# Weighing a pair of items together in split precision, in a neighbourhood attention on one core

## The chip, the core and the metric

The kernel runs on one core of a Trainium2 chip. TensorE (PE) multiplies matrices from the on-chip memory SBUF into the accumulators PSUM (eight banks of 128 x 512 float32). VectorE (DVE), ScalarE (ACT) and GpSimd (POOL) compute on both or on SBUF; SyncE (SP) issues the DMAs. Each engine takes its own instructions strictly in order and waits for others on semaphores. The metric is the device time of one execution in microseconds; the median over runs is reported.

## The reference

One layer of a hybrid encoder, applied with shared weights to a prompt of 512 tokens and a sample of 1024 tokens, width 1024, all float32. The part that matters here is group B, a two-dimensional neighbourhood attention with 8 heads of 64 on a grid of 64 columns:

```python
def _neighbourhood_attention(q, k, v, rpb):
    ...
    r_start = jnp.clip(r_idx - kh // 2, 0, rows - kh)
    ...
    def row_fn(args):
        r, r0, q_row = args
        k_strip = lax.dynamic_slice_in_dim(kg, r0, kh, axis=1)
        v_strip = lax.dynamic_slice_in_dim(vg, r0, kh, axis=1)
        ...
        sc = jnp.einsum('bqhd,bikhd->bhqik', q_row, k_strip,
                        preferred_element_type=jnp.float32) * scale + bias[None]
        sc = jnp.where(col_ok[None, None, :, None, :], sc, -jnp.inf)
        p = jax.nn.softmax(sc.reshape(b, h, GRID_W, kh * GRID_W), axis=-1)
        ...
        return jnp.einsum('bhqik,bikhd->bqhd', p, v_strip)
```

Group A is a plain attention of 8 query heads over 2 key heads. Input projection, output projection, a gated MLP with a short convolution, an embedding gate and norms surround the two.

## The kernel before

The kernel runs in five stages; the attention is the second (`s2_*`), one function for each engine. Activations lie transposed, features on partitions. Between the stages all engines meet (`end_stage`). Matrix products outside group B's weighing are made from numbers in the type float32r, split into a rounded part and the remainder (names that end in H and L, `three_pass`).

The attention goes over 8 pairs of heads, four of group A (p = 0 to 3) and four of group B (p = 4 to 7). A pair is 24 items: two heads (`s`), each with three blocks (`g`: the prompt's 512 queries, the two halves of the sample's 1024), each of four items of 128 queries (`item`). An item of group B is two grid rows of 64 queries. The keys of the two rows overlap: `window` gives 512 keys where both rows have the same first key row ("edge", four blocks of 128), otherwise 576 ("mid", four blocks of 128 and one of 64). The three blocks of a head have 4 edge items; 2 edge and 2 mid; 2 mid and 2 edge.

`every_pair` calls `step` for m = 0 to 23 on each engine, so the order on each engine is fixed. In step m of group B:

- PE: `scores` of item m + 2 (L944, L945), `turn` of item m (L955: transposes of the probabilities into PSUM banks 4 and 5, after the exponential of m and once both banks are free), and in even steps `weigh_step` for items m - 2 and m - 1 (L979), from step 2 on; `norm_row` (L963) when m % 4 == 3. In steps 6 and 23 `values` (L929) turns the values of a head through the same two banks.
- ACT: `turned` copies bank 0 to PF (L1052), then `exps` of item m + 2 (L1042), and a `square` at steps 3, 19 and 23.
- DVE: `row_max` of item m + 2 (L1145: adds the bias table and finds the maximum), `turned_low` copies bank 1 to PF (L1154). If m % 4 == 1 it first reads out the finished output block, `out` (L1173 a copy of the accumulators to H, L1175 a multiplication by the inverse row sums), and takes `turned_low` ahead of `row_max`. Steps 3 to 5 and 18 to 20 also build bias tables (L1114, L1118, L1119).

Group A has the same steps, with both parts of the number: ACT copies both banks rounded to PTH (L1054), DVE then subtracts that from the bank and writes the remainder to PTL (L1158), and only that frees the bank (`t_hi`, `t_free`). Its `weigh` (L985) multiplies 128 x 128 values (64 columns rounded part, 64 remainder) with 256 columns of probabilities, two items at once, with PTH and with PTL. The output then comes in two halves of the partitions, so `out_copy` (ACT, L1061) takes one half out of PSUM and DVE adds the other (L1178) before it multiplies (L1182). In group B the values are float32 and 64 columns wide, the probabilities float32 and each item is weighed by itself in 128 columns; such a product is recorded twice in the trace.

## Time and profile before

| | |
|---|---|
| median of 3 runs | 2393.69 us (2391.83 to 2396.62) |
| profiled execution | 2396.31 us, its span 2394.2 us |
| mean granted TensorE clock | 0.975 |
| PE busy | 94% of the span |
| DVE, ACT, POOL busy | 68%, 34%, 12% |
| attention of group A, 372 to 672 us | PE busy 252.8 us of 300 |
| attention of group B, 672 to 905 us | PE busy 229.2 us of 233 |

The span runs from the first to the last instruction of the profiled execution; its time is a little more. Busy times are of one engine; matmuls overlap in a pipeline, so a busy PE need not be at its peak. The granted clock is the share of TensorE's full clock.

### The profile page before, as it was taken

The numbers are of one execution on the slowest core, as the hardware profiler recorded it, in microseconds if no ns is written. First come the engines' busy times: TensorE is split into PE (matmuls) and PEld (weight loads), VectorE is DVE, ScalarE is ACT, GpSimd is POOL, SyncE is SP. The second block draws the span as 40 slices with busy tenths as digits, with TensorE's granted clock in tenths as the row PEclk, the third lists the DMA queues.
The fourth block names the chain that finished last, engine by engine and source line by source line (L and its number), as shares of the span: only waits on it lengthen the run. The fifth ranks groups of instructions, "written<-read, shape, count | busy, mean of one in ns | idle before, by whom it ended". The sixth has DMA issues, their size and how long they took to land.

```text
span 2394.2 us, 30366 instructions
## 1 busy us (share of the span) xinstructions
PE 2247.9 (94%) x11036; PEld 1842.2 (77%) x11036; DVE 1621.3 (68%) x2130; ACT 802.1 (34%) x1281; POOL 297.7 (12%) x184
## 2 busy tenths in 40 slices
PE   6999998888899998998999999999999999987996
PEld 4777876777777787777888888888888888876884
DVE  7677427777766664774777776777777776775545
ACT  5222107666755553132121221122211222134223
POOL 6101010000000000540000000000000000014100
PEclk9999999999999998998999999999999999997997
DMA  5223445101045523010110000000000100010102
GB/s 164 101 83 115 152 143 121 27 13 26 15 89 108 108 54 123 35 36 18 36 35 26 35 35 26 35 35 26 35 35 26 35 35 26 35 53 18 44 27 105
DMA packets 51020, 137.47 MB, mean 57 GB/s; under 512 B 20240, under 2 KB 20752, under 8 KB 50960
## 3 DMA queue, kind: packets, MB, share of 16 engines
q1 hardware_dynamic: 50096, 135.55, 18.7%
q10 hardware_dynamic: 864, 1.13, 0.1%
q8 instruction: 37, 0.61, 0.1%
q14 instruction: 23, 0.19, 0.0%
HBM read 105.99 MB, written 30.67 MB: 57 GB/s over the span
## 4 chain that ended last, share of the span: by engine, by line
PE 68%; issue 23%; DVE 4%; POOL 2%; ACT 1%; DMA 1%; SPq 0%; POOLq 0%; ACTq 0%; DVEq 0%
PE ps L297 22%; PE ps L298 22%; PE ps L299 22%; POOL acc_a L915 1%; DVE WL L293 1%; POOL acc_b L915 1%; DVE NL L629 1%; PE ps L485 1%; PE ps L480 1%; DVE NL L1733 1%; DMA raw<-in_w 0%; DVE NL L1414 0%; DVE H L1905 0%; DMA ident<-in_ident 0%; PE ps L1244 0%
## 5 line engine op out<-in xcount | busy, mean ns | idle before, releaser
L297 PE MATMUL ps<-NH,WH 128*128 128x512 f32 x1896 | 756.8, 399 | 44.3 <-DVE WL L293 30.8
L298 PE MATMUL ps<-NL,WH 128*128 128x512 f32 x1896 | 743.5, 392 | 0.0
L299 PE MATMUL ps<-NH,WL 128*128 128x512 f32 x1896 | 742.8, 392 | 0.0
L297 PEld LDWEIGHTS ps<-NH,WH 128*128 128x128 f32 x1896 | 359.6, 190 | 129.4 <-issue 36.2
L298 PEld LDWEIGHTS ps<-NL,WH 128*128 128x128 f32 x1896 | 359.5, 190 | 79.9 <-issue 6.0
L299 PEld LDWEIGHTS ps<-NH,WL 128*128 128x128 f32 x1896 | 359.1, 189 | 76.0
L1665 DVE TENSOR_TENSOR H<-H,ps 128x512 f32<-128x512 f32 x480 | 305.4, 682 | 106.6 <-PE ps L299 106.6
L274 POOL TENSOR_TENSOR raw<-raw,gains 128x1024 f32<-128x1024 f32 x78 | 156.3, 2009 | 1378.7 <-DMA raw<-in_w 1368.2
L289 ACT ACTIVATE WH<-raw 128x1024 fp32r<-128x1024 f32 x104 | 109.9, 1057 | 574.9 <-PE ps L299 548.8
L955 PE MATMUL ps<-ident,PR 128*128 128x128 f32 (+1 forms) x1056 | 164.5, 285 | 49.8 <-DVE PTL L1158 45.0
L297 PE MATMUL ps<-MH,WH 128*128 128x512 f32 x504 | 197.9, 393 | 4.7 <-DVE H L1740 4.5
L299 PE MATMUL ps<-MH,WL 128*128 128x512 f32 x504 | 197.1, 391 | 0.0
L955 PEld LDWEIGHTS ps<-ident,PR 128*128 128x128 f32 (+1 forms) x1056 | 120.2, 141 | 99.8 <-DVE PTL L1158 54.8
L298 PE MATMUL ps<-ML,WH 128*128 128x512 f32 x504 | 196.9, 391 | 0.0
L293 DVE TENSOR_TENSOR WL<-raw,WH 128x1024 fp32r<-128x1024 f32 x104 | 133.8, 1287 | 52.4 <-ACT WH L289 52.4
L1647 DVE SCALAR_TENSOR_TENSOR ca<-u,convw,ca 128x511 f32<-128x511 f32 x88 | 113.1, 1343 | 43.3 <-ACT ca L1573 43.3
L1647 DVE SCALAR_TENSOR_TENSOR cg<-u,convw,cg 128x511 f32<-128x511 f32 x84 | 107.0, 1332 | 43.6 <-ACT cg L1573 43.6
L1137 DVE TENSOR_REDUCE nmax<-ps 128x1 f32<-128x1024 f32 (+1 forms) x96 | 99.2, 1033 | 41.6 <-PE ps L945 36.5
L297 PEld LDWEIGHTS ps<-MH,WH 128*128 128x128 f32 x504 | 94.9, 188 | 28.6 <-DVE H L1740 9.3
L1054 ACT ACTIVATE PTH<-ps 128x512 fp32r<-128x512 f32 (+1 forms) x192 | 94.1, 525 | 51.1 <-PE ps L955 50.0
L299 PEld LDWEIGHTS ps<-MH,WL 128*128 128x128 f32 x504 | 95.0, 189 | 19.8
L298 PEld LDWEIGHTS ps<-ML,WH 128*128 128x128 f32 x504 | 95.1, 189 | 19.3
(166 smaller groups left out, 2814.9 us busy)
## 6 DMA issues: line engine op xcount, KB each, us to landing
raw<-in_w SPq DMA_DIRECT2D x102, 512.0 KB, 3.2
xst<-in_xT SPq DMA_DIRECT2D x24, 256.0 KB, 4.3
H<-in_xT SPq DMA_DIRECT2D x8, 768.0 KB, 10.4
out_yT<-H SPq DMA_DIRECT2D x24, 256.0 KB, 2.1
qkh<-oqh SPq DMA_DIRECT2D x5, 768.0 KB, 3.3
qkl<-oql SPq DMA_DIRECT2D x5, 768.0 KB, 4.9
qkh<-obh SPq DMA_DIRECT2D x5, 768.0 KB, 3.5
qkl<-obl SPq DMA_DIRECT2D x5, 768.0 KB, 6.0
```

Of the source, the lines that this page charges most:

```text
L274: nc.gpsimd.tensor_tensor(v, v, g, ALU.mult).then_inc(w_sc, 1)
L289: nc.scalar.activation(WH[:, slot, :], raw[:, slot, :], ACT.Copy).then_inc(w_hi, 1)
L293: nc.vector.tensor_tensor(WL[:, slot, :], raw[:, slot, :], WH[:, slot, :].bitcast(F32), ALU.subtract).then_inc(w_lo, 1)
L297: nc.tensor.matmul(out, wh, xh, start=first, stop=False)
L298: nc.tensor.matmul(out, wh, xl, start=False, stop=False)
L299: return nc.tensor.matmul(out, wl, xh, start=False, stop=last)
L915: nc.gpsimd.tensor_tensor(v, v, sqo[:], ALU.add).then_inc(o_acc, 1)
L955: mm = nc.tensor.transpose(ps[0:kn, TBANK + b, cols(j, P)], src, ident[:, :])
L1054: nc.scalar.activation(turned_dst(PTH, m, w, b), src, ACT.Copy).then_inc(t_hi[b], 1)
L1137: nc.vector.tensor_reduce(nmax[:, m:m + 1], score_bank(m, w), AXX, ALU.min).then_inc(m_done, 1)
L1647: nc.vector.scalar_tensor_tensor(buf[:, to_], u[:, from_], convw[:, bass.ds(f, 1), w:w + 1].rearrange("p a b -> p (a b)"), buf[:, to_], AL ...
L1665: nc.vector.tensor_tensor(h, h, ps[:, DOWN_BANKS[c], :], ALU.add).then_inc(h_add, 1)
```

## The change

Group B gets what group A has. Values are kept in VT as rounded part and remainder (128 columns), probabilities in PTH and PTL; ACT copies both banks, DVE subtracts in both, and `out_copy` joins the two halves of the output; in group B ACT does that copy at the start of its step, ahead of `turned`. `weigh` handles two items in one call. Their windows may be shifted by one block of 128 keys: `pair_blocks` lists the key blocks that both have in full (256 columns, both items) and then those that belong to one item (128 columns). To that end the turned blocks of an item with a shifted window are stored one place further on (`shift`, `turned_dst`). `split_blocks` now cuts the list of blocks in two halves in order, so the block of 64 keys is in bank 1 and no longer in bank 0.

```diff
         def split_blocks(w):
 
             b = key_blocks(w)
-            h = len(b) // 2
-            return [b[:h] + b[2 * h:], b[h:2 * h]]
...
+            h = (len(b) + 1) // 2
+            return [b[:h], b[h:]]
+
+        def shift(kind, m):
+
+            return (window(kind, m)[0] - window(kind, m - m % 2)[0]) // P
+
+        def pair_blocks(kind, m):
+
+            even, odd = ({shift(kind, x) + kb: kn for kb, kn in key_blocks(window(kind, x)[1])} for x in (m, m + 1))
+            both = [(n, even[n], 0, 2 * P) for n in even if odd.get(n) == even[n]]
+            own = [(n, x[n], at, P) for x, y, at in ((even, odd, 0), (odd, even, P)) for n in x if y.get(n) != x[n]]
+            return both + own
...
-                todo = places(w)
-                c0 = (m % 2) * P
-                if kind == "B":
-                    for kb, kn, n in todo:
-                        mm = nc.tensor.matmul(ps[0:DH, PVBANK, at:at + queries], VF[s][0:kn, k0 // P + kb, 0:DH],
-                                              PF[0:kn, (m // 2) % 2, n, c0:c0 + queries],
-                                              start=kb == 0, stop=kb == todo[-1][0])
-                    return mm
...
+                todo = pair_blocks(kind, m)
+                for x, (n, kn, c0, queries) in enumerate(todo):
+                    for t in (PTH, PTL):
+                        mm = nc.tensor.matmul(ps[:, PVBANK, at + c0:at + c0 + queries], VT[s][0:kn, k0 // P + n, :],
+                                              t[0:kn, (m // 2) % 2, n, c0:c0 + queries],
+                                              start=(x == 0 and t is PTH), stop=(t is PTL and x == len(todo) - 1))
                 return mm
...
             def step(kind, p, i, m, before, after):
                 own = kind if m > 1 else before
                 over = read_out(kind, p, m, before, False)
+                if over and own == "B":
+                    out_copy(*over)
                 if i is None:
                     return
                 turned(kind, p, m, 0)
-                if kind == "A":
-                    turned(kind, p, m, 1)
-                else:
-                    act.wait_ge(t_rdy[1], fills(kind, p, ("T", m)))
+                turned(kind, p, m, 1)
...
             def turned_low(kind, p, m, b):
 
                 _, w, _, _ = window(kind, m)
-                if kind == "B":
-                    dve.wait_ge(t_rdy[1], fills(kind, p, ("T", m)))
-                    nc.vector.tensor_copy(turned_dst(PF, m, w, 1),
-                                          turned_src(1, len(split_blocks(w)[1]))).then_inc(t_free[1], 1)
-                    return
...
-                if kind == "B":
-                    dve.wait_ge(pv_done, p * 6 + b + 1)
-                    dve.wait_ge(r_rdy, p * 6 + b + 1)
-                    dst = H[rows, bass.ds(p, 1), cols(g)].rearrange("p a n -> p (a n)")
-                    nc.vector.tensor_copy(dst, ps[0:DH, PVBANK, :]).then_inc(o_sum, 1)
-                    dve.wait_ge(o_sum, p * 6 + b + 1)
-                    nc.vector.tensor_tensor(dst, dst, ps[rows, RBANK, :], ALU.mult).then_inc(o_done, 1)
-                    return
...
                     late = own == "B" and m % 4 == 1
                     if late:
+                        turned_low(kind, p, m, 0)
                         turned_low(kind, p, m, 1)
```

## Rows read from the trace of the kernel before

**Rows 1.** The page, busy time of an engine, share of the span, instructions.

```profile
PE 2247.9 (94%) x11036; PEld 1842.2 (77%) x11036; DVE 1621.3 (68%) x2130; ACT 802.1 (34%) x1281; POOL 297.7 (12%) x184
```

**Rows 2.** Windows, attention of A and of B: stretch, length, busy by engine, clock, DMA.

```profile
core 0: us, PE busy (x) PEld busy (x) DVE busy (x) ACT busy (x) POOL busy (x), PEclk, DMA share, GB/s
...
372.00:672.00 300.00, 252.82 (x1702) 213.69 (x1700) 229.87 (x364) 206.59 (x417) 16.71 (x13) 0.98 0.17 37
672.00:905.00 233.00, 229.17 (x1662) 186.32 (x1662) 151.87 (x385) 117.89 (x296) 16.07 (x12) 1.00 0.41 83
```

**Rows 3.** Windows, weighing to weighing in one B head pair, from "4 to 6".

```profile
735.58:741.38 5.80, 4.83 (x35) 3.81 (x34) 5.08 (x9) 1.76 (x5) 1.27 (x1) 1.00 0.00 0
741.38:747.04 5.66, 5.66 (x49) 5.02 (x48) 4.14 (x13) 3.95 (x10) 0.00 (x0) 1.00 0.00 0
...
752.17:757.36 5.19, 5.19 (x37) 4.07 (x37) 2.46 (x10) 2.95 (x9) 0.00 (x0) 1.00 1.03 238
757.36:761.63 4.27, 4.12 (x29) 3.19 (x28) 2.98 (x7) 1.50 (x5) 0.00 (x0) 1.00 1.02 224
761.63:766.14 4.51, 4.51 (x35) 3.96 (x34) 2.50 (x10) 3.09 (x9) 0.00 (x0) 1.00 1.13 187
...
770.54:775.27 4.73, 4.73 (x37) 4.18 (x36) 3.83 (x12) 3.47 (x9) 0.00 (x0) 1.00 0.00 0
775.27:780.53 5.26, 5.21 (x34) 3.65 (x33) 4.64 (x9) 1.98 (x5) 1.27 (x1) 1.00 0.09 19
780.53:786.98 6.45, 6.45 (x50) 4.99 (x49) 3.14 (x11) 3.99 (x11) 0.25 (x1) 1.00 1.00 230
...
sum 60.32, PE 58.88 PEld 47.49 DVE 40.16 ACT 30.53 POOL 3.81; mean PE 4.91 PEld 3.96 DVE 3.35 ACT 2.54 POOL 0.32
```

**Rows 4.** Timeline of B: start, us, engine, line, operation, idle before and releaser.

```profile
759.47 0.68 DVE L1173 COPY H<-ps 64x512 f32 x1 [1.25 <-PE ps L979]
...
760.19 0.68 DVE L1175 TENSOR_TENSOR H<-H,ps 64x512 f32 x1
...
761.13 0.67 DVE L1145 CUSTOM_DVE_ANT_0 SC<-ps,TE 128x512 f32<-128x512 f32 x1
...
761.63 1.96 PE L979 MATMUL ps<-PF,VF 128*64 128x128 f32 x16
...
761.85 0.72 ACT L1042 ACTIVATE PR<-SC,nmax 128x512 f32<-128x512 f32 x1 [1.23 <-DVE nmax L1145]
...
763.52 0.50 PE L944 MATMUL ps<-KH,Q 128*128 128x512 f32 x1
...
775.27 2.82 PE L979 MATMUL ps<-PF,VF 128*64 128x128 f32 x20
```

**Rows 5.** Timeline of A: its read-out, turned copies and subtractions, and a weighing.

```profile
468.66 0.59 ACT L1061 ACTIVATE osum<-ps 64x512 f32<-64x512 f32 x1 [0.22 <-PE ps L985]
...
469.28 0.68 DVE L1178 TENSOR_TENSOR osum<-ps,osum 64x512 f32<-64x512 f32 x1 [0.97 <-ACT osum L1061]
...
470.11 0.68 DVE L1182 TENSOR_TENSOR H<-osum,ps 64x512 f32 x1
...
476.35 0.66 ACT L1054 ACTIVATE PTH<-ps 128x256 fp32r<-128x256 f32 x2 [1.75 <-PE ps L955]
...
476.77 0.76 DVE L1158 TENSOR_TENSOR PTL<-ps,PTH 128x256 fp32r<-128x256 f32 x2
...
477.25 0.77 PE L955 MATMUL ps<-ident,PR 128*128 128x128 f32 x4 [0.25 <-DVE PTL L1158]
...
477.77 0.36 PE L985 MATMUL ps<-PTH,VT 128*128 128x256 f32 x1
...
484.18 0.38 PE L985 MATMUL ps<-PTH,VT 128*128 128x256 f32 x1
...
485.11 0.28 PE L985 MATMUL ps<-PTL,VT 128*128 128x256 f32 x1
```

**Rows 6.** Groups by line and shape, A's window: the wide subtraction, busy and mean ns.

```profile
L1158 DVE TENSOR_TENSOR PTL<-ps,PTH 128x512 fp32r<-128x512 f32 x128 | 82.2, 680 | 1.6 <-ACT PTH L1054 0.5
```

**Rows 7.** Line L1114 (bias table), what it waited for: us in total, times.

```profile
  DMA TR<-in_rpb: 3.4, 3
```

More of the change, by code:

```diff
@@ L189, in build @@
         QS, KH, KL = ({"A": [x, y], "B": [z, y]} for x, y, z in ((QA0, Q1, QB0), (KHA0, KH1, KHB0), (KLA0, KL1, KLB0)))
-        value_home = c.at
         VT = [c(f"VT{s}", [T // P, P], F32R) for s in range(2)]
-        probs_home = c.at
         PTH = c("PTH", [2, TS // P, 2 * P], F32R)
-        VF = [nc.alloc_sbuf_tensor_at(f"VF{s}", [P, T // P, DH], F32, offset=value_home + 6 * KB * s) for s in range(2)]
-        PF = nc.alloc_sbuf_tensor_at("PF", [P, 2, TS // P, 2 * P], F32, offset=probs_home)
         PTL = c("PTL", [2, TS // P, 2 * P], F32R)
@@ L965, in norm_row, with weigh @@
                 mm.then_inc(r_rdy, 1)
-            def weigh(kind, p, b, m, queries):
+            def weigh(kind, p, b, m):
                 s = b // 3
-                k0, w, _, _ = window(kind, m)
+                k0, _, _, _ = window(kind, m)
                 at = (m % 4) * P
-                pe.wait_ge(t_free[0], fills(kind, p, ("T", m + queries // P - 1)) + T_FREE)
-                pe.wait_ge(t_free[1], fills(kind, p, ("T", m + queries // P - 1)) + T_FREE)
+                for bank in range(2):
+                    pe.wait_ge(t_free[bank], fills(kind, p, ("T", m + 1)) + T_FREE)
@@ L983, in weigh @@
-                for kb, kn, n in todo:
-                    for x in (PTH, PTL):
-                        mm = nc.tensor.matmul(ps[:, PVBANK, at:at + queries], VT[s][0:kn, k0 // P + kb, :],
-                                              x[0:kn, (m // 2) % 2, n, c0:c0 + queries],
-                                              start=(kb == 0 and x is PTH), stop=(kb == todo[-1][0] and x is PTL))
+                todo = pair_blocks(kind, m)
[4 more added lines that the diff above has]
+                                              start=(x == 0 and t is PTH), stop=(t is PTL and x == len(todo) - 1))
@@ L988, in weigh @@
                 return mm
             def weigh_step(kind, p, m):
-                if kind == "A" and m % 2 == 1:
-                    mm = weigh(kind, p, (m - 3) // 4, m - 3, 2 * P)
-                    if m % 4 == 1:
-                        mm.then_inc(pv_done, 1)
-                if kind == "B" and m % 2 == 0:
-                    weigh(kind, p, (m - 2) // 4, m - 2, P)
-                    mm = weigh(kind, p, (m - 2) // 4, m - 1, P)
-                    if m % 4 == 0:
+                lag = 3 if kind == "A" else 2
@@ L1000, in weigh_step @@
+                if (m - lag) % 2 == 0:
+                    mm = weigh(kind, p, (m - lag) // 4, m - lag)
+                    if (m - lag) % 4 == 2:
                         mm.then_inc(pv_done, 1)
@@ L1029, in values @@
             def values(kind, p, s):
-                if kind == "B":
-                    act.wait_ge(t_rdy[0], fills("B", p, ("V", s)))
-                    nc.scalar.activation(VF[s][:, 0:6, 0:DH], value_src(0), ACT.Copy).then_inc(t_free[0], 1)
-                    return
                 for b in range(2):
-                    act.wait_ge(t_rdy[b], fills("A", p, ("V", s)))
+                    act.wait_ge(t_rdy[b], fills(kind, p, ("V", s)))
                     nc.scalar.activation(VT[s][:, 6 * b:6 * b + 6, 0:DH], value_src(b), ACT.Copy).then_inc(t_hi[b], 1)
@@ L1050, in turned @@
                 src = turned_src(b, len(split_blocks(w)[b]))
-                if kind == "B":
-                    nc.scalar.activation(turned_dst(PF, m, w, b), src, ACT.Copy).then_inc(t_free[b], 1)
-                else:
-                    nc.scalar.activation(turned_dst(PTH, m, w, b), src, ACT.Copy).then_inc(t_hi[b], 1)
+                nc.scalar.activation(turned_dst(PTH, kind, m, w, b), src, ACT.Copy).then_inc(t_hi[b], 1)
             def out_copy(p, b):
@@ L1197, in step @@
                     if not late:
-                        if kind == "A":
-                            turned_low(kind, p, m, 0)
+                        turned_low(kind, p, m, 0)
                         turned_low(kind, p, m, 1)
```

23 lines of the change are left out of this document (6 added, 17 removed).

## Prediction, before the result was known

> **What bounds the kernel now.** I read the page first, for the whole. TensorE (PE) is busy 94% of the span [rows 1]: the kernel is a TensorE kernel, but that is an average over stages. The windows by stage come next, because the change touches one stretch alone, group B's attention from 672 to 905 us. There PE is busy 229.2 of 233 us at a granted clock of 1.00, VectorE (DVE) 151.9, ScalarE (ACT) 117.9; in group A's attention just ahead of it PE is busy 252.8 of 300, DVE 229.9, ACT 206.6, clock 0.98 [rows 2]. A already runs as B will after the change: each turned bank is copied by ACT, then subtracted by DVE, before PE may refill it. So B's rows say what is given up and A's rows what takes its place.
>
> Third, the windows from one weighing of a B pair of heads to the next, twelve to a head pair of 24 items: 60.3 us, of it PE 58.9, DVE 40.2, ACT 30.5 [rows 3]. Even here two kinds differ. An interval that holds the read-out of an output block (steps with m % 4 == 1) has PE idle for a moment (4.12 of 4.27); one without has it busy throughout (4.51 of 4.51). A call "k to k+2" is the interval from the weighing in step k to the next.
>
> **What the change removes from PE.** A weighing of two items over the same four key blocks is 16 records of L979 (8 products, two records each), and 1.89 us pass from its start to the next scores (761.63 to 763.52); one over five blocks each is 20 records, busy 2.82 where the 16 are busy 1.96, so 2.75 [rows 4]. Now the first is 4 blocks x 2 parts = 8 products of 256 columns. The same 8 in group A start 0.93 apart from first to last (484.18 to 485.11), so 1.05 to the next work at their pitch of 0.12 [rows 5]: saved 0.84. A pair whose windows are shifted has 3 shared blocks (6 products of 256 columns) and 4 own ones (8 of 128 columns). A 128-column product in this number format is not in the trace. Bounds: half of A's pitch for half the columns, 0.06, and the two records that such a product took before at (1.96 - 0.28) / 15 = 0.112 each, 0.22. I take 0.12, as A's, the nearest row with this stationary side: 14 products, 1.77 us, saved 1.0. A head pair has 8 of the first kind and 4 of the second: 8 x 0.84 + 4 x 1.0 = 10.7 us less PE work, 43 us for the four head pairs. Were PE still the bound, that would be the gain.
>
> The Trainium skill ("TensorE: Matmul & The Clock Gate", section LDWEIGHTS) says a weight load costs by its columns, so the stationary side growing from 64 to 128 columns doubles it to about 107 ns; by that rule the own products could not come near 0.06, and the sum of loads alone would rise (832 x 53 ns to 480 x 107 ns, an estimate from the page). The pitches of 0.112 with 64 columns and 0.12 with 128 show no such doubling; in both the products may cover the load.
>
> **What it adds.** Per item: on ACT a second copy (bank 1), 0.28 behind another [rows 5]; on DVE a subtraction of bank 0, 0.33 behind another for 256 columns, and by the 512-column group [rows 6] some 0.47 for 384 (8 of 24 items). Per output block: an ACT copy of the low half, 0.62 with its handover. The DVE copy becomes an addition of the same length. Values: one more pass each on ACT and DVE, twice a head pair. Sums for a head pair: DVE 16 x 0.33 + 8 x 0.47 + 2 x 0.47 = 10.0, so 50.2; ACT 24 x 0.28 + 6 x 0.62 + 2 x 0.4 = 11.2, so 41.7; PE 58.9 - 10.7 = 48.2. The three are now near each other, and each is served by the others in turn, so the handovers set the pace. Moving the 64-row block from bank 0 to bank 1 costs nothing, since each bank is read as wide as before. No DMA is added or moved.
>
> **The interval with a read-out**, from the start of the weighing (0). The last of 8 products starts at 0.93 and ends at 1.21; ACT copies at 1.25; DVE adds 0.62 later (468.66 to 469.28), at 1.87, multiplies 0.83 later (469.28 to 470.11) at 2.70, and 0.60 after that the first subtraction starts, 3.30 [rows 5]. In step m % 4 == 1 both subtractions wait behind the read-out on DVE, PE's next turn waits for them, and the next weighing is queued behind that turn. Two subtractions are 0.76, and the weighing starts 0.24 after them (476.77 + 0.76 = 477.53, 477.77) [rows 5]: 4.30. Before: DVE's copy starts 2.11 after the weighing (757.36 to 759.47), the multiply 0.72 later, and one bank copy follows: 4.27 to the next weighing [rows 3, 4]. So the whole 0.84 saved is used up by the ACT copy (0.62), the slower add-to-multiply (0.11) and the second subtraction: no gain in such an interval.
>
> **The interval without.** The first subtraction of the step before started at -1.00 from the new weighing; row_max(3) follows the second at -0.32; its exponential starts 0.72 later (761.13 to 761.85) [rows 4], at 0.40; ACT's turned copies of the item come behind it in ACT's order, at 1.12; DVE subtracts 0.42 after the copy's start (476.35 to 476.77), 1.54; inverse 2.21, row_max(5) 2.35, subtractions of item 3 at 2.96, done 3.72, weighing at 3.96. PE's own work in it (weighing 1.05, two scores and turns 1.8, norm row 0.43) is only 3.3 us and lies inside. Against 4.51 [rows 3]: 0.5 gained. This chain (row_max, exponential, copy, subtraction) is what is late next.
>
> The same walk with the special steps put in: a mixed weighing that ends 0.7 later and 384-column subtractions (+0.14) make a read-out interval 5.15 (two of them; before 5.26 in one, next to nothing gained); three plain ones 4.3; 10 to 12 4.1 (before 5.2); 14 to 16 4.0; 2 to 4 4.05; 18 to 20, three 576-column items and two table steps on DVE, 5.1 (before 4.7, a loss); 4 to 6 5.0 (before 5.80). In 4 to 6 the kernel before loses time to the bias table's DMA, 3.4 us in 3 such waits [rows 7]; that DMA starts after the last scores of the head pair and lands as late after them whatever the change does. The steps between it and its use stay about as long in my walk, so a wait stays, but it lies beside the longer ACT and DVE work of the steps and costs some 0.5 us in place of 1.1. Where values are turned (6 to 8 and 22 to 0), a third fill of the two banks must pass through copy and subtraction: a 0.47 copy, 0.04, two subtractions of 0.55 overlapping to 1.0, against one copy on each engine side by side. I get 6.4 for 6 to 8 (before 5.66) and 6.1 for 22 to 0 (before 6.45, a mixed weighing). Sum: 3 x 4.3 + 2 x 5.15 + 4.1 + 4.0 + 4.05 + 5.1 + 5.0 + 6.4 + 6.1 = 57.95 against 60.32. For four head pairs 2.4 x 4 = 9.5 us less. I take off 1.5 us for handovers that I rounded down and the longer last read-out: 8 us.
>
> **Rivals.**
> Handovers eat it: a mean of 0.2 us more in each of 12 intervals than walked makes 2.4 us per head pair, all of the gain; then about 2394. For it: A, built this way, waits for DVE's subtraction again and again, 0.25 us on PE in the row at 477.25 [rows 5]. Against: the walk takes each handover from those very rows.
> Slower: the own 128-column products cost as the two records did, 0.22 each. A mixed weighing then takes 2.6 us, 0.9 more; in all four mixed intervals of a head pair that lies on the path (the read-out, or the turn behind the scores, is late by as much): 3.6 x 4 = 14 us, 2400. It decides (more than 0.2% slower) from about 0.21 us each. Against it: L979's two records belong to the plain format.
> The clock: with PE's work at 48 of 58 us, the granted clock falls as in A, 0.98 [rows 2], or further. If a tenth of PE's work, 4 x 48 x 0.1 = 19 us, ran at 1.2 GHz instead of 2.4, it would take 19 us more; PE's idle 10 of 58 us hide little of it where the work is dense: 2386 + 19 = 2405. It decides from 13 us, 7% of the work. A's waits left 0.98, and B's are shorter. The Trainium skill ("TensorE: Matmul & The Clock Gate", Part 1) says that the clock drops to half after PE stands idle for a while, which speaks against trading PE work for waits.
> PE stays the bound: if DVE and ACT slot in beside it, 2394 - 43 = 2351. For it: DVE has 20 us of 60 idle now [rows 3]. Against: ordering, as walked.
>
> **The numbers.** The profiled execution took 2396.3 us, span 2394.2, 2.1 outside; the median of runs is 2393.7. The sum is a difference, so it is taken from the median: 2393.7 - 8 = 2386. What a measurement can tell from no change is 0.2%, 4.8 us. Forecast (walk right within 0.1 us an interval, 4.8 us in all): 0.53, a seventh of it above 2389; handovers eat it 0.27, a quarter of that slower than 2398.5; own products double 0.08; clock 0.05; PE bound 0.07. Faster 0.45 + 0.07 = 0.52; same 0.08 + 0.20 = 0.28; slower 0.07 + 0.08 + 0.05 = 0.20. The range must reach to the case that eats the gain and to the double price: 2376 to 2402; the forecast's own is 2380 to 2392. PE-bound and the clock's far end stay out.
>
> **What would show it.** L985 in B with 352 records of 256 and 128 of 128 columns, pitch 0.12 for both (else the second rival). Stretch of B 225 us instead of 233, PE busy about 80% of it, DVE 85%. PE's turns wait for DVE's subtraction. Read-out intervals 4.3, plain ones 4.0, value steps above 6. PEclk 1.00. The prediction is wrong if plain intervals are over 4.2, if the exponential is not what ACT's turned copy waits behind, or if the table's DMA lands later than now.

## The result, and the profile after

The changed kernel takes 2402.16 us (median of 20 runs, 2398.42 to 2407.87), the kernel before in the same series 2396.77 us (20 runs, 2391.83 to 2403.79). The ratio is 1.0023 with a 95% interval of 1.0015 to 1.0031: 5.4 us slower, where 8 us faster were forecast. 2402.16 is also just above the range's upper end, 2402.

First the page of the kernel after, busy time of each engine, to be held against [rows 1]:

```profile
PE 2216.1 (92%) x10684; PEld 1817.9 (76%) x10684; DVE 1657.9 (69%) x2234; ACT 845.6 (35%) x1409; POOL 297.3 (12%) x184
```

PE lost 31.8 us of work, DVE gained 36.6, ACT 43.5. PE's saving is there, smaller than the 43 us forecast, and the time went up. Next the windows of the kernel after, columns as in [rows 2]: group B's stretch, then one B head pair from weighing to weighing (steps 0 to 2, 2 to 4 and so on to 22 to 0), with its sum.

```profile
672.00:905.00 233.00, 191.46 (x1282) 157.50 (x1281) 182.50 (x475) 157.43 (x413) 14.46 (x11) 0.98 0.41 83
...
730.34:734.92 4.58, 3.09 (x22) 2.39 (x22) 3.50 (x9) 2.53 (x7) 0.96 (x1) 1.00 1.01 205
734.92:739.03 4.11, 3.80 (x28) 3.11 (x28) 3.09 (x11) 3.71 (x11) 0.00 (x0) 1.00 0.74 101
739.03:745.17 6.14, 4.17 (x28) 3.61 (x27) 5.32 (x13) 2.96 (x8) 1.58 (x1) 0.89 0.00 0
745.17:751.32 6.15, 6.03 (x42) 4.99 (x41) 5.21 (x14) 4.78 (x12) 0.00 (x0) 0.83 0.00 0
751.32:756.77 5.45, 4.42 (x30) 3.44 (x28) 3.75 (x9) 2.83 (x7) 0.00 (x0) 1.00 0.20 60
756.77:761.48 4.71, 4.71 (x32) 3.79 (x32) 3.43 (x12) 3.58 (x11) 0.00 (x0) 1.00 1.04 228
761.48:765.93 4.45, 3.10 (x23) 2.40 (x22) 3.41 (x9) 2.62 (x7) 0.00 (x0) 1.00 1.03 222
765.93:769.97 4.04, 3.73 (x28) 3.08 (x27) 3.15 (x12) 3.47 (x10) 0.00 (x0) 1.00 1.15 182
769.97:774.79 4.82, 3.43 (x28) 3.11 (x27) 3.76 (x9) 2.78 (x7) 0.00 (x0) 1.00 0.14 18
774.79:779.74 4.95, 4.02 (x32) 3.35 (x29) 4.31 (x13) 4.06 (x11) 0.00 (x0) 1.00 0.00 0
779.74:785.32 5.58, 4.44 (x30) 3.44 (x28) 4.96 (x12) 3.10 (x8) 1.29 (x1) 1.00 0.24 62
785.32:791.99 6.67, 6.01 (x45) 4.65 (x44) 4.45 (x14) 5.11 (x14) 0.33 (x1) 1.00 1.01 220
...
sum 61.65, PE 50.95 PEld 41.35 DVE 48.34 ACT 41.51 POOL 4.16; mean PE 4.25 PEld 3.45 DVE 4.03 ACT 3.46 POOL 0.35
```

In these 233 us PE is busy 191.5 us instead of 229.2, but the changed kernel's group B runs on past 905 us, so this is no like for like. From A's last weighing to B's last, PE is busy 197.5 of 241.3 us after and 230.3 of 234.7 before: 33 us less work in 6.6 us more (225 us were forecast for the stretch of 233). This head pair takes 61.65 us, PE 50.95 of it, against 60.32 and 58.88 [rows 3]; the walk, the prediction's sum of the twelve intervals, had 57.95 and 48.2. Read the same way from PE's timeline, the four head pairs can be laid side by side. Most intervals repeat within 0.03 us (those of the last head pair within 0.3) and stand once, as in the second and third. Three at the ends of B differ, since A's work lies ahead of them or nothing behind: 0-2 and 2-4 of the first head pair (4.38 and 3.45 after) and 22-0 of the last (3.91 after). In 1, 8-10 varies from 4.28 to 4.76. "4 to 6" and "6 to 8" do not repeat, and their sum is given for each of the four. The rows further down are of the experiments, by their numbers; each row is one profiled execution. 15 holds 5's repeats too.

| kernel | 0-2 | 2-4 | 8-10 | 10-12 | 12-14 | 14-16 | 16-18 | 18-20 | 20-22 | 22-0 | 4 to 8, head pairs 1 to 4 |
|---|---|---|---|---|---|---|---|---|---|---|---|
| the walk | 4.30 | 4.05 | 5.15 | 4.10 | 4.30 | 4.00 | 4.30 | 5.10 | 5.15 | 6.10 | 11.40 each |
| before | 4.39 | 4.52 | 5.13 | 5.19 | 4.27 | 4.51 | 4.40 | 4.74 | 5.26 | 6.44 | 10.04, 11.46, 10.53, 10.27 |
| after | 4.58 | 4.07 | 5.46 | 4.71 | 4.45 | 4.04 | 4.82 | 4.95 | 5.58 | 6.67 | 11.55, 12.29, 11.94, 12.53 |
| 2, bank copies old | 4.12 | 3.59 | 4.99 | 4.43 | 4.30 | 3.48 | 4.49 | 3.85 | 5.11 | 6.33 | 10.48, 15.25, 15.17, 12.57 |
| 3, read-out old | 3.80 | 4.05 | 4.92 | 4.71 | 3.66 | 4.04 | 3.85 | 4.95 | 4.97 | 6.67 | 12.24, 15.18, 12.89, 15.27 |
| 1, both old | 3.46 | 3.59 | 4.40 | 4.44 | 3.33 | 3.47 | 3.46 | 3.85 | 4.61 | 6.33 | 11.84, 14.62, 15.45, 12.41 |
| 12, both old, early table | 3.46 | 3.59 | 4.36 | 4.44 | 3.32 | 3.48 | 3.46 | 3.84 | 4.61 | 6.33 | 10.37, 11.65, 11.30, 10.19 |
| 7, early table | 4.58 | 4.08 | 5.46 | 4.72 | 4.44 | 4.05 | 4.82 | 4.95 | 5.58 | 6.66 | 11.55, 12.49, 11.39, 12.50 |
| 11, padded, early table | 4.58 | 4.06 | 4.81 | 3.93 | 4.55 | 4.05 | 4.82 | 4.95 | 5.08 | 5.89 | 11.55, 11.39, 11.36, 11.34 |
| 15, and deferred | 4.42 | 4.05 | 4.82 | 3.93 | 4.29 | 4.05 | 4.42 | 4.95 | 5.08 | 5.89 | 11.25, 12.32, 12.32, 12.15 |
| 16, and covered | 4.43 | 4.11 | 4.83 | 3.93 | 4.29 | 4.04 | 4.44 | 4.93 | 5.08 | 5.88 | 11.17, 11.02, 11.15, 11.11 |

After less walk, four head pairs: the intervals with a mixed weighing (8-10, 10-12, 20-22, 22-0) 1.92 x 4 = 7.7 us; the other read-out intervals (0-2, 12-14, 16-18) 0.95 x 4 = 3.8; 4 to 8 2.7; the rest about -0.4. Sum 13.8. The row "before" shows one thing more. The walk took 60.32, the second head pair's time, for all four; but in the others 4 to 8 is 10.04, 10.53 and 10.27 instead of 11.46, and four head pairs of this row make 237.7 us and not 4 x 60.32 = 241.3. So 3.6 of the 9.5 us forecast were not there to be gained. By the rows after less before is -9.5 + 3.6 + 13.8 = 7.9 us; the intervals at the ends of B take 1.3 off, which leaves the 6.6 measured in the two profiled executions. (Their spans are 8.8 us apart, where the medians are 5.4 apart; 2.4 of the 8.8 is there before B: A's last weighing starts at 670.27 instead of 667.84.)

The waits of the kernel after in B (who waited for whom, us in total, times, longest) show what most of PE's free time is: it stands before a turn and waits for DVE's subtraction.

```profile
PE ps L957 <- DVE PTL L1132: 36.7, 38, 1.7
DVE osum L1144 <- ACT osum L1045: 22.8, 25, 1.9
ACT PTH L1038 <- PE ps L957: 17.3, 36, 1.6
DVE PTL L1132 <- ACT PTH L1038: 12.9, 23, 1.1
DVE TE L1097 <- DMA TR<-in_rpb: 0.8, 2, 0.6
```

The timeline of PE in the kernel after shows a plain weighing at the lower clock after a long wait, and the own products of a mixed one; the columns are start, duration, engine, line, operation, then the idle time ahead and its releaser.

```profile
744.19 1.33 PE L957 MATMUL ps<-ident,PR 128*128 128x128 f32 x5 [1.69 <-DVE PTL L1132]
745.17 0.56 PE L980 MATMUL ps<-PTH,VT 128*128 128x256 f32 x1
745.53 0.42 PE L980 MATMUL ps<-PTL,VT 128*128 128x256 f32 x1
745.75 0.41 PE L980 MATMUL ps<-PTH,VT 128*128 128x256 f32 x1
...
752.11 0.22 PE L980 MATMUL ps<-PTH,VT 128*128 128x128 f32 x1
752.17 0.28 PE L980 MATMUL ps<-PTL,VT 128*128 128x128 f32 x1
752.38 0.32 PE L980 MATMUL ps<-PTH,VT 64*128 64x128 f32 x1
752.54 0.27 PE L980 MATMUL ps<-PTL,VT 64*128 64x128 f32 x1
752.74 0.33 PE L980 MATMUL ps<-PTH,VT 128*128 128x128 f32 x1
...
753.48 0.50 PE L946 MATMUL ps<-KHB,QB 128*128 128x512 f32 x1
```

The weight loads of the same products (PEld):

```profile
752.12 0.19 PEld L980 LDWEIGHTS ps<-PTL,VT 128*128 128x128 f32 x1
752.38 0.18 PEld L980 LDWEIGHTS ps<-PTH,VT 64*128 64x128 f32 x1
752.49 0.19 PEld L980 LDWEIGHTS ps<-PTL,VT 64*128 64x128 f32 x1
752.74 0.19 PEld L980 LDWEIGHTS ps<-PTH,VT 128*128 128x128 f32 x1
752.85 0.19 PEld L980 LDWEIGHTS ps<-PTL,VT 128*128 128x128 f32 x1
```

From 752.11 to the next scores at 753.48 the 8 own products take 1.37 us, 0.17 each, where 0.12 was taken. The first two, with 128 rows, are 0.06 apart; at each step from 128 rows to 64 or back the next starts 0.20 later, and the second of the two behind such a step 0.16. The loads tell it more plainly: 0.11 apart where the rows stay the same, be they 128 or 64, and 0.25 or 0.26 where they change. The whole mixed weighing takes 753.48 - 751.32 = 2.16, forecast 1.77. Near 745 the products are 0.21 apart and more instead of 0.12.

### The profile page after: what moved, and what is told of

It is laid out like the page before. It is cut to its first block, busy times and chain, and to the rows that moved or that the text cites. A ratio compares the mean times of both kernels' runs of the same rounds, so it can differ in the third digit from the quotient of the medians.

```text
span 2403.0 us, 29856 instructions
## 1 busy us (share of the span) xinstructions
PE 2216.1 (92%) x10684; PEld 1817.9 (76%) x10684; DVE 1657.9 (69%) x2234; ACT 845.6 (35%) x1409; POOL 297.3 (12%) x184
## 4 chain that ended last, share of the span: by engine, by line
PE 68%; issue 24%; DVE 4%; POOL 2%; ACT 1%; DMA 1%; SPq 0%; POOLq 0%; ACTq 0%; DVEq 0%
PE ps L293 22%; PE ps L294 22%; PE ps L295 22%; POOL acc_a L917 1%; DVE WL L289 1%; POOL acc_b L917 1%; DVE NL L625 1%; PE ps L481 1%; PE ps L476 1%; DVE NL L1699 1%; DVE NL L1380 0%; DMA raw<-in_w 0%; DVE H L1871 0%; DMA ident<-in_ident 0%; PE ps L1210 0%
## 5 line engine op out<-in xcount | busy, mean ns | idle before, releaser
L1132 DVE TENSOR_TENSOR PTL<-ps,PTH 128x256 fp32r<-128x256 f32 (+2 forms) x384 | 183.1, 516 | 15.7 <-ACT PTH L1038 13.4
L1038 ACT ACTIVATE PTH<-ps 128x256 fp32r<-128x256 f32 (+2 forms) x384 | 161.1, 460 | 70.4 <-PE ps L957 68.2
L980 PE MATMUL ps<-PTH,VT 128*128 128x256 f32 (+2 forms) x560 | 155.0, 307 | 2.0 <-DVE H L1148 1.3
L980 PE MATMUL ps<-PTL,VT 128*128 128x256 f32 (+2 forms) x560 | 143.8, 289 | 0.0
```

The costliest lines, as they stand in the source:

```text
L980: mm = nc.tensor.matmul(ps[:, PVBANK, at + c0:at + c0 + queries], VT[s][0:kn, k0 // P + n, :], t[0:kn, (m // 2) % 2, n, c0:c0 + queries], ...
L1038: nc.scalar.activation(turned_dst(PTH, kind, m, w, b), src, ACT.Copy).then_inc(t_hi[b], 1)
L1132: nc.vector.tensor_tensor(turned_dst(PTL, kind, m, w, b), turned_src(b, len(split_blocks(w)[b])), turned_dst(PTH, kind, m, w, b).bitcast(F ...
```

## The experiments

All ratios are against the kernel before, run in the same series (its medians 2395.7 to 2397.1); a us figure worked out from a ratio is the ratio's distance from 1 times 2397.

**1. Both handovers as before** (l1_both_old). PE's new products stay, ACT copies bank 0 and DVE bank 1 again, without a subtraction (the rounded part is multiplied twice in place of the remainder of the probabilities), and DVE reads out the block alone (the half of the sum with the values' remainder is left out). The turned values still pass through copy and subtraction. **2. Only the bank copies as before** (l2_bank_old) and **3. only the read-out as before** (l3_read_old) are its two halves.

```diff
                 turned(kind, p, m, 0)
-                turned(kind, p, m, 1)
+                if kind == "A":
+                    turned(kind, p, m, 1)
+                else:
+                    act.wait_ge(t_rdy[1], fills(kind, p, ("T", m)))
...
+                if kind == "B":
+                    if b == 1:
+                        dve.wait_ge(t_rdy[1], fills(kind, p, ("T", m)))
+                        nc.vector.tensor_copy(turned_dst(PTH, kind, m, w, 1),
+                                              turned_src(1, len(split_blocks(w)[1]))).then_inc(t_free[1], 1)
+                    return
...
-                if over and own == "B":
-                    out_copy(*over)
...
+                    nc.vector.tensor_copy(dst, ps[0:DH, PVBANK, :]).then_inc(o_sum, 1)
```

> The changed kernel with its new products, but both handovers of the kernel before: ACT copies bank 0 and DVE bank 1 (no subtraction for the probabilities; the rounded part is multiplied twice, so the number and shape of the products stay), and the output is read out by DVE alone from the lower 64 partitions. The remainders of probabilities and values are thereby left out of the result. Theory H (the handovers between engines took the gain): about 40 us less PE work and nothing against it, so some 2356 to 2365. Theory P (the products are the trouble: own products of 0.17 us and PE's clock at 1.2 GHz): the handovers are of no account, within 6 us of the changed kernel, 2396 to 2408.

> As the run with both handovers old, but with the changed kernel's read-out (ACT copies the upper half, DVE adds, then multiplies). The remainder of the probabilities is left out of the result. Theory H: the subtraction costs 0.35 us in each read-out interval, 0.6 in each other one and about 1 where values are turned, so without it 24 us or so less than the changed kernel: 2378. Theory P: 2396 to 2408.

> The changed kernel with the old read-out alone (DVE copies the lower 64 partitions and multiplies; the products with the values' remainder are computed and left out of the result). Theory H: 0.62 us of ACT copy and 0.11 of the add-to-multiply go from each of 24 read-out intervals, 17 us: 2385. Theory P: 2396 to 2408.

Measured: both 2373.52 us, 0.9908 [0.9893, 0.9922]; bank copies alone 2390.78, 0.9981 [0.9972, 0.9991]; read-out alone 2394.50, 0.9995 [0.9984, 1.0006]. Against the changed kernel the bank copies give 10 us, the read-out 7, both together 27.5 and not 17. The table of intervals resolves this. Outside 4 to 8 a head pair is shorter by 4.7 us with the bank copies old, by 3.7 with the read-out old, by 8.4 with both: the parts add up. What doesn't repeat is 4 to 8, whose four sums are 48.3 us after, and 53.5, 55.6 and 54.3 in these three: each variant pays 5 to 7 us there, and both together pay it once. So the handovers hold the time: undoing them alone, with PE's new products in place, makes the kernel 22 us faster than before. It is short of the 2356 to 2365 of the theory, and much is lost in 4 to 8. The windows, the DVE timeline and the waits of the variant with both say what that is:

```profile
672.00:905.00 233.00, 209.63 (x1366) 178.57 (x1366) 159.32 (x399) 125.83 (x314) 18.04 (x14) 0.92 0.41 83
...
731.18:734.06 2.88, 0.44 (x5) 0.20 (x4) 1.78 (x5) 0.36 (x1) 0.06 (x1) 1.00 0.01 1
...
736.43:743.50 7.07, 7.07 (x37) 6.46 (x36) 4.68 (x13) 4.40 (x10) 0.00 (x0) 0.52 0.00 0
```

```profile
732.16 0.62 DVE L1101 SCALAR_TENSOR_TENSOR TE<-TR,colmask 128x448 f32<-128x448 f32 x1 [3.31 <-DMA TR<-in_rpb]
```

```profile
DVE TE L1101 <- DMA TR<-in_rpb: 9.4, 3, 3.3
```

Once the steps are faster, the bias table, whose transfer is issued at the same place, is late by 9.4 us in three waits; PE idles behind it (0.44 busy of 2.88, of it 2.44 waiting for DVE's copy) and then runs 7 us at a granted clock of 0.52. Experiment 12 tests this.

**4. Add, both subtractions, multiply** (i1_interleave): the DVE's read-out is split, so that PE's turn is served before the multiply.

```diff
                 nc.vector.tensor_tensor(osum[rows, :], ps[0:DH, PVBANK, :], osum[rows, :], ALU.add).then_inc(o_sum, 1)
+                between()
...
+                def lows():
                     if late:
                         turned_low(kind, p, m, 0)
                         turned_low(kind, p, m, 1)
+
+                if over and own == "B":
+                    out("B", *over, lows)
```

> The changed kernel, complete, with one order altered on DVE: in the steps with a read-out the two subtractions stand between the addition and the multiplication, not behind both. Theory H: PE's turn no longer waits for the multiplication, but the next weighing still does (it needs the accumulators free), so 0.3 us of each of 24 read-out intervals: 7 us less, 2395. Theory P: no change, 2402.

Measured: 2405.47 us, 1.0045 [1.0032, 1.0057]: 5 us slower than the change, not faster. PE's turn comes earlier and the read-out intervals are shorter (12-14 4.01), but the next weighing now waits for the multiplication, and the intervals behind are longer (14-16 4.24). Outside 4 to 8 a head pair still gains 0.5 us, 2.2 in all; 4 to 8 loses 4.7 us, and PE spends 20 us of B at half the clock, not 10. PE's timeline of this variant, start of a weighing:

```profile
767.76 0.38 PE L980 MATMUL ps<-PTH,VT 128*128 128x256 f32 x1 [0.16 <-DVE H L1149]
```

**5. Scores repeated to keep PE busy** (f1_filler): the first 512 columns of the scores of every fourth item are multiplied three times instead of once, in the steps with m % 4 == 2.

```diff
-                for c0 in range(0, w, GT):
+                for c0 in [*range(0, w, GT)] + [0] * (2 if kind == "B" and m % 4 == 0 else 0):
```

> The changed kernel, complete; in steps with m % 4 == 2 of group B the first 512 columns of the next scores are multiplied three times over instead of once (the last result stands), so that PE works some 0.95 us more just where it waits 1.4 to 1.7 us for the subtraction. Theory C (part of the loss is PE's clock, three stretches of 3.4 us at 1.2 GHz in group B): no such stretch is left, and at most 1.6 us each comes back, 3 to 5 us: 2398. Theory H (the handovers alone): no change, 2402. If PE were the bound: 24 x 0.95 = 23 us more, 2425.

Measured: 2400.16 us, 1.0020 [1.0011, 1.0029]; B's clock 0.99. Not to be told from the change's 1.0023. In the second head pair the repeats fill part of the wait ahead of the turn in step 6, which was 1.69 us and is now 0.69:

```profile
743.71 0.77 PE L957 MATMUL ps<-ident,PR 128*128 128x128 f32 x5 [0.69 <-DVE PTL L1132]
```

Two of the three stretches at half the clock are gone, in the second and third head pair, and yet 4 to 8 takes 12.39 and 11.81 there instead of 12.29 and 11.94: in these two, where the table is late as well, taking the slow clock away gained nothing that the run shows. The third stretch stayed, behind a wait of 1.33 us ahead of the values' turns, which the repeats don't reach; 6-8 is 7.76 there.

**6. Own products left out** (o1_no_own): the 8 products of each mixed weighing are not made, so these blocks' share of the sum is missing.

```diff
-            return both + own
+            return both + own if kind == "A" else both
```

> The changed kernel with the own products of shifted pairs left out (8 of 14 in each of 16 weighings; the result lacks those keys). The trace has them at 0.17 us each, 1.37 a weighing. Theory H with the products on the path to the read-out: 1.3 us from each of the 8 weighings with a read-out behind, and some 0.4 from the 8 others: 14 us less, 2388. If the products lay beside the handovers everywhere: under 3 us.

Measured: 2390.01 us, 0.9979 [0.997, 0.9988]: 10.5 us less than the change, where 14 were expected. A mixed weighing is 1.36 us shorter (0.80 instead of 2.16), 22 us for 16, and only half of that comes through: 8-10, 10-12, 20-22 and 22-0 are 4.73, 3.88, 5.09 and 5.84, 2.9 us a head pair less than after, 12-14 is 0.15 longer.

**7 and 8. The bias table's transfer issued earlier**, ahead of the last scores of the head pair before, in the changed kernel (t1_table_early) and in the kernel before (t0_before_table_early).

```diff
                 for s in range(2):
+                    load_table(i, s)
                     scored(i + (NPAIR_A - 1), s)
...
                     load_values("B", i, s)
-                    load_table(i, s)
```

> The changed kernel, complete, with the bias table's DMA issued ahead of the queries and keys and ahead of the wait for the last scores. The trace of the changed kernel has 0.8 us of waits for it left in two places, so theory H: under 1 us, 2401. If that transfer paced the head pair (17 us from the last scores to the table): up to 6 us less.

> The kernel before, with the table's DMA issued as early. Its trace has three waits of 3.4 us in all on DVE, and PE idle 0.75 us behind one: 2 to 3 us less than before, 2393.5. None of it if PE catches up.

Measured: 2400.11 us, 1.0016 [1.0007, 1.0025], and 2392.85, 0.9987 [0.9979, 0.9996]: 1.7 us less than the change, and 3 us less than the kernel before. (In the kernel before, 4 to 8 took 10.03 in every head pair with the early table; what the wait cost it was 1.4, 0.5 and 0.2 us in the last three.) In the changed kernel the wait is gone, but 6 to 8 now has the slow clock in two head pairs, 7.78 instead of 6.61, and these 2.3 us take the place of most of the gain.

**9. Shared block of 64 keys padded to 128** (o2_shared4): columns of zero probability fill the short block, so that all products have 128 rows and a mixed weighing has 4 shared blocks and one own block each, 8 products of 256 columns and 4 of 128.

```diff
-            h = (len(b) + 1) // 2
+            b = [(k, P) for k, _ in b]
+            h = (len(b) + 1) // 2
...
+                nc.gpsimd.memset(PR[:, x, 9 * GRID:10 * GRID], 0.0).then_inc(zeroed, 1)
```

> The changed kernel, complete, but the block of 64 keys is treated as a full one whose upper 64 probabilities are zeros (64 columns of PR are zeroed once), so that a shifted pair shares four blocks instead of three: 8 products of 256 columns and 4 of 128, no change between 128 and 64 rows, instead of 6 and 8. From the pitches of the changed kernel's trace, 8 x 0.12 + 4 x 0.16 = 1.6 us instead of 2.16. Theory H with the own products on the path (as the run without them showed, 12 us for 1.37 us each): a little under half of that, 5 us: 2397. If only their number of rows mattered elsewhere: 2402.

Measured: 2394.62 us, 0.9993 [0.9983, 1.0003], 7.2 us less than the change and equal to before. The timeline of PE in this kernel has the own products with equal rows:

```profile
750.67 0.22 PE L989 MATMUL ps<-PTH,VT 128*128 128x128 f32 x1
750.73 0.28 PE L989 MATMUL ps<-PTL,VT 128*128 128x128 f32 x1
750.84 0.27 PE L989 MATMUL ps<-PTH,VT 128*128 128x128 f32 x1
750.95 0.27 PE L989 MATMUL ps<-PTL,VT 128*128 128x128 f32 x1
```

0.06 and 0.11 apart. So the 0.17 was not the price of 128 columns but of the rows; that it is the change of rows, and not the 64, is told by the loads above, since no run used 64 rows alone. A mixed weighing takes 1.43 us instead of 2.16, 0.73 less; the intervals are 0.65, 0.78, 0.50 and 0.78 shorter (table of intervals, 11 against after) and 12-14 0.10 longer, so nine tenths of it reach the end. Leaving out the rest of the own products as well, as in 6, gives hardly more: another 0.63 us a weighing shortens these intervals by 0 to 0.07. From there on the handovers hold them. That the median fell by only 7.2 and not by 10 us is in 4 to 8 again: it took 14.68 us in one head pair of the profiled execution.

**10. Padding, early table and filler together** (c1_all), and **11. without the filler** (c3_pad_early).

> The changed kernel, complete, with the three aids together: four shared blocks, the bias table's DMA early, the scores of every fourth item multiplied three times over to keep PE at work. If they add up (5, 2 and 2 us): 2393, still no faster than the kernel before with the early table (2393). If they overlap: 2397.

> Four shared blocks and the early table alone, without the repeated scores. If what keeps PE's clock up gives 2 us here too, 2392; if with fewer and shorter waits the clock stays up by itself, 2390.

Measured: 2389.88 us, 0.9973 [0.9961, 0.9985], and 2391.63, 0.9976 [0.9967, 0.9985]. Both do the whole computation, and both beat the kernel before by some 6 us. With the padding in, the early table is worth 0.9993 - 0.9976, 4 us; the padding and it together leave B's clock at 1.00, and 4 to 8 at 11.4.

**12. Both handovers as before, early table** (l4_both_old_early): experiment 1 with the edit of 7. **13. The same with one product per block** (n1_rounded): the rounded parts alone are multiplied.

```diff
-                    for half, t in enumerate((PTH, PTL if kind == "A" else PTH)):
+                    for half, t in (((0, PTH), (1, PTL)) if kind == "A" else ((1, PTH),)):
```

> The kernel with the new products and both old handovers (remainders left out of the result as there), which came to 2373.5, now with the bias table's DMA early. Its trace has 9.4 us of waits for that DMA on DVE, up to 3.3 at once, and PE at 1.2 GHz for 24 us in group B. Theory: that is where the rest of the 43 us of PE work went, so 10 to 14 us less, 2360 to 2364. If the handovers of the scores and exponentials hold the rest: under 4 us less, 2370.

> As the last, and each key block multiplied once, with the rounded part alone (the remainders of probabilities and values are left out, so the result is less precise): PE has 1040 x 0.12 us or so less still, some 5 us a head pair. If PE is still the bound with the table early: 2345. If the handovers and the clock hold it by now: within 5 us of the run before it.

Measured: 2362.84 us, 0.9856 [0.9838, 0.9873], within what was expected, and 2353.13, 0.9824 [0.9801, 0.9846], 8 us above it. Windows and waits of the first of the two:

```profile
672.00:905.00 233.00, 211.88 (x1410) 179.95 (x1409) 168.43 (x412) 135.90 (x333) 18.08 (x14) 0.94 0.39 83
```

```profile
PE ps L958 <- DVE PTH L1141: 5.8, 14, 0.8
```

34.5 us come through, of 38 by which PE's busy time in B is shorter here (192.4 for 230.3, last weighing of A to last of B), once PE waits for DVE only 5.8 us instead of 36.7. Halving the number of products adds 8 more; by then B's granted clock is 0.86 and PE waits 15 us for DVE and ACT before its turns of the probabilities.

**14. ACT's exponential behind the read-out copy** (r1_defer), and **15. that in the version of 10** (c2_all_defer). ACT has the exponential of the next item ahead of the block's copy, here in the kernel after, ACT's and then DVE's timeline:

```profile
770.72 0.78 ACT L1029 ACTIVATE PR<-SC,nmax 128x576 f32<-128x576 f32 x1
...
771.61 0.59 ACT L1045 ACTIVATE osum<-ps 64x512 f32<-64x512 f32 x1
772.23 0.66 ACT L1038 ACTIVATE PTH<-ps 128x256 fp32r<-128x256 f32 x2
```

```profile
772.24 0.69 DVE L1144 TENSOR_TENSOR osum<-ps,osum 64x512 f32<-64x512 f32 x1 [0.89 <-ACT osum L1045]
773.06 0.69 DVE L1148 TENSOR_TENSOR H<-osum,ps 64x512 f32 x1
773.79 0.76 DVE L1132 TENSOR_TENSOR PTL<-ps,PTH 128x256 fp32r<-128x256 f32 x2
```

The weighing starts at 769.97; by the walk the copy would start 1.25 later, at 771.22. It starts at 771.61, behind the exponential, and DVE waits 0.89 us for it.

```diff
-                if m + 2 < ITEMS:
+                put_off = kind == "B" and (m >= 4 or before == "B")
+                if put_off and m % 4 == 1:
+                    exps(kind, p, m + 1)
+                if put_off and m % 4 == 0:
+                    pass
+                elif m + 2 < ITEMS:
                     exps(kind, p, m + 2)
```

> The changed kernel, complete, with one order altered on ACT: the exponential that ACT issues in a step with m % 4 == 0 is put behind the read-out's copy and the two turned copies of the next step. In the changed kernel's trace that exponential ends up to 0.4 us after the weighing, so the copy, the addition and all behind them start late. If the walk missed just that: 24 x 0.2 to 0.4 us, 5 to 9 us less, 2395. If the exponential, now later itself, holds up DVE or PE instead: no change, 2402, or slower.

> The run with the three aids (2389.9) with that order on ACT as well: 2382 if the first theory holds, 2390 or more otherwise.

Measured: 2403.03 us, 1.0024 [1.0015, 1.0033], against 1.0023, and 2390.76, 0.9973 [0.9963, 0.9984], against 0.9973: by the times, nothing. By the intervals, something else: 15 against 10 has 0-2, 12-14 and 16-18 shorter by 0.16, 0.26 and 0.40, 4-6 by 0.23 (4.77 to 4.54), some 1.0 a head pair, and 6-8 at half the clock in three of four (7.78, 7.78 and 7.67) instead of 6.61, 3.4 us more. Gain and loss nearly cancel. Two more runs test that.

**16. Deferred, and the wait covered** (w1_defer_warm), with **17. the covering alone** (w2_warm) as its control: five products whose result nobody reads, into the bank of the norm row, in the 1.42 us in which PE waits ahead of the values' turns; padding and early table in both, no other filler.

```diff
                 if m == V1_AT and kind == "B":
+                    s, g, t, _ = item(m)
+                    q = QS[kind][s][:, g * GT + t * P:g * GT + (t + 1) * P].bitcast(F32R)
+                    for _x in range(5):
+                        nc.tensor.matmul(ps[:, RBANK, :], q, KH[kind][s][:, 0:GT].bitcast(F32R),
+                                         start=True, stop=True)
                     values("B", p, 1)
```

> Padding, early table and the exponential behind the read-out copy, and five repeated products of 512 columns into the bank of the norm row between the weighing of step 6 and the turns of the values, where PE otherwise waits 1.42 us. Theory C (the deferred exponential does shorten the read-out intervals, by 0.15 + 0.26 + 0.40 + 0.23 us a head pair as the traces of versions 10 and 15 show, and what eats the gain is a stretch at half the clock behind that wait, 7.78 us for 6 to 8 instead of 6.61 in three head pairs): 6 to 8 is 6.61 in all four, and the time is some 3.5 to 4 us below the padded versions without deferring, 2386 to 2387 (0.9958 or so). Theory N (deferring gains nothing, the clock costs nothing): 2390 to 2391, as the two versions before.

> The same repeated products in the version with padding and early table alone, where the clock was 1.00 already. Both theories: no change against that version, 2390 to 2392 (0.9976); if the repeated products delay the values' turns, 6 to 8 grows above 6.61 and the time by up to 1 us.

Measured: 2385.57 us, 0.9965 [0.9953, 0.9977], and 2389.25, 0.9976 [0.9967, 0.9985] (before 2395.74). PE's timeline of 16 has the wait nearly filled:

```profile
740.63 0.94 PE L938 MATMUL ps<-ident,vraw 64*128 64x64 f32 x12 [0.26 <-DVE PTL L1151]
```

6-8 is 6.61 in all four head pairs, as in 11, and the deferring keeps its gain: the four head pairs together take 224.9 us instead of 228.8 in the control, 3.9 less, the medians 3.7. The intervals of the two ratios overlap, but each of 16's 6 runs is below each of the control's 11. The control is equal to 11, as both theories had it. Version 16 does the whole computation and is the fastest of those that do: 8.4 us below the kernel before by its ratio, 10.2 by the medians. That is not all the change's: the early table alone takes 3 us off the kernel before (experiment 8), and against that version 16 is ahead by 5 us.

## Why the prediction was wrong

**What bounds the kernel, and what comes after it: right.** PE was the bound and is no longer: busy 82% of B's stretch ("about 80%" was said; DVE 78%, 85% was said), and its turns wait 36.7 us for DVE's subtraction. Experiments 1 and 12 show that the handovers hold the time. The sums of work were near: in the head pair above DVE 48.3 us (50.2 was said), ACT 41.5 (41.7), PE 50.95 (48.2).

**The base: wrong, 3.6 us.** The gain of a head pair, 2.4 us, was read off the second one and taken four times. That pair had the longest wait for the bias table; the others had 0.9 to 1.4 us less to give.

**Plain intervals: right**, 4.04 and 4.07 for 4.0 and 4.05. That a plain read-out interval gains nothing was right as well; it loses. 4 to 8 was right where nothing disturbs it, 11.34 to 11.55 for 11.4.

**The term of the own products: wrong, and the largest part, 7.7 us.** It was priced at 0.12 each, the pitch of 256-column products, with 0.22 as upper bound; measured 0.17. The nearest row misled because in it all products have 128 rows; here they alternate between 128 and 64, and that, not the columns, costs (0.06 to 0.11 with equal rows, experiment 9). The weighing is 0.39 longer, 6.2 us for 16, and the intervals with it lose a little more. The rows before had a sign of it: in [rows 4] the weighing of 20 records is busy 0.86 longer than that of 16, 0.215 for each of the four more, which have 64 rows, where the prediction reckoned 0.112 a record. The rival that doubled the price had the place and the path right (experiment 9: at this length of the weighing nine tenths of what it gets shorter reach the end; experiment 6: below 1.43 us hardly anything does) and its reason wrong. The Trainium skill's rule for weight loads ("TensorE: Matmul & The Clock Gate", section LDWEIGHTS: the cost goes by columns) does not tell these cases apart; here loads of the same 128 columns come 0.11 us apart with equal rows and 0.25 to 0.26 where the rows change.

**The read-out interval, 4.30: 0.15 to 0.52 too short, 3.8 us.** The walk let ACT's copy of the block start 0.04 after the last product. On ACT the next item's exponential lies ahead of it, and the copy starts 0.39 later than walked (771.61 for 771.22); in 0-2 and 12-14 it is 0.14. Put behind the copy, the exponential gives back 0.15, 0.16 and 0.38 of these intervals (16 against after), 2.8 us of the 3.8. The walk had checked DVE's queue for what stands ahead of the read-out, and not ACT's. The last 1 us is in the step from the multiplication to the first subtraction. The walk had 0.60, and named [rows 5] for it, where no row has it. In the read-outs of a pair's first head it is that (12-14: 0.60), in those of the second 0.72 or 0.73 (773.06 to 773.79; so in 0-2 and 16-18), and it stays so when the exponential is put off: 2 x 0.12 x 4 = 1.0 us. Why the second head's take longer no run shows.

**The table's wait and the clock, 2.7 us in 4 to 8: wrong.** "PEclk 1.00" was wrong: in three head pairs PE waits 1.3 to 1.7 us in step 6 and runs some 3.5 us at half its clock. Where nothing else is late there, such a stretch costs 1.17 us (7.78 against 6.61); in the kernel after that is so in the last head pair (7.69), while in the second and third, beside the table's wait, taking it away gave nothing (experiment 5). So the clock costs 1 to 3.5 us in these versions, not the rival's 19. The table's wait alone costs about what was taken (0.5 us a head pair; 1.7 us in all came back in 7). What was not seen is that the two, with the late copy, lie at one place: removing one alone (7, 14) left stretches at half the clock in two and three head pairs, and the gain came through in 11 and 16, where none was left.

**Which rival won:** none alone makes 2402. Of the 17.4 us by which the rows miss the 9.5 forecast by the walk, 7.7 are the own products', 3.8 the read-outs' ("handovers eat it" had that place), 2.7 lie in 4 to 8, with the clock in them, and 3.6 in the base, which no rival had; the rest is -0.4. The walk took the shortest handover seen for most steps, so nearly all errors went one way (18 to 20, 4.95 for 5.10, went the other); 0.53 for "right within 0.1 us an interval" didn't allow for that. The three signs of being wrong that were named did not come: plain intervals are under 4.2, the exponential is what ACT's copy stands behind there, and the table's wait fell from 3.4 to 0.8 us. None of them watched the read-out or the mixed weighing.

## What to carry to other kernels

Work taken off the busiest engine is worth only what the ring of the other engines lets through: here 33 us less on PE, paid with one more dependent step on two engines at two places, came to 5 us more, and came to 40 us less than that with the two steps undone and the table early. In walking such a ring, list every queue ahead of each handover, ACT's too, and where products of full and half row counts alternate on PE, try padding: here it gave 7 us. Before a gain is multiplied by the repetitions, look whether they are alike; here one of four head pairs was read, and it was the odd one. When several small losses lie at one place, times of single removals say little: compare interval by interval, and remove them together.

## What the runs showed of the hardware

Products in this number format with 128 columns are 0.06 and 0.11 us apart when all have 128 rows (experiment 9), and 0.20 to 0.21 at each change between 128 and 64 rows, 0.16 for the next behind it. Their weight loads are 0.11 apart with equal rows and 0.25 to 0.26 at a change. Filling up the short block with zeros was 7.2 us faster than using it short. The granted clock was about half in the 3.5 us behind a stretch of 4 us in which PE had waited 1.7 us (busy 2.22 of it); the windows of the kernel after around that place:

```profile
740.00:744.00 4.00, 2.22 (x14) 1.70 (x13) 3.49 (x8) 2.12 (x5) 0.98 (x1) 0.98 0.00 0
744.00:747.50 3.50, 3.19 (x16) 2.89 (x17) 3.44 (x11) 2.25 (x6) 0.00 (x0) 0.53 0.00 0
747.50:751.00 3.50, 3.50 (x29) 2.74 (x29) 2.63 (x8) 2.35 (x8) 0.00 (x0) 1.00 0.00 0
```

That is the lower of its two levels, 1.2 GHz of 2.4. The Trainium skill ("TensorE: Matmul & The Clock Gate", Part 1) says that the clock drops to half after idleness; the trace agrees, with 1.69 us of idle time ahead of 744.19. But the padded kernel with an early table (11) has waits of 1.35 and 1.42 us in step 6 of the second head pair and keeps 1.00, while 15 has there only the one of 1.42 and loses it: the wait alone doesn't decide it.
